# Block 2's experts: rows gathered by index, thirteen weight places, results added to the residual at once

## What is computed

```
def ec_moe(h, w_router, w_gate, w_up, w_down):          # h: 512 tokens x 1024
    cap = EC_FACTOR * T // N_EXPERTS_2                   # 2 * 512 // 16 = 64
    aff = softmax(h @ w_router)                          # 512 x 16
    wts, tok = lax.top_k(swapaxes(aff, 1, 2), cap)       # each expert picks its 64 tokens
    xs = h[bidx, tok]                                    # 16 x 64 x 1024
    hid = silu(xs @ w_gate[e]) * (xs @ w_up[e])          # 1024 x 2048 each
    y = (hid @ w_down[e]) * wts                          # 2048 x 1024
    return zeros_like(h).at[bidx, tok].add(y)

    h2 = modulate(rms_norm(x, norm_ffn_g), sh2, sc2)
    x = x + g2 * ec_moe(h2, ...)
    out = rms_norm(x, norm_final_g)
```

## Time and profile before

| | us |
|---|---|
| median of three runs | 3543.57 |
| lowest and highest run | 3541.1, 3547.78 |
| the profiled execution's own time | 3537.41 |
| its span in the trace | 3535.6 |
| mean granted clock of PE, share of full | 0.92 |

### The profile page before, as it was taken

One profiled execution on the slowest core, in us unless ns is written; L12 is line 12 of the kernel. 1 busy time (PEld: TensorE's weight loads), 2 busy tenths in 40 slices (PEclk: granted clock), 3 DMA queues, 4 the chain that ended last, 5 costly groups with the idle time before them and its releaser, 6 DMA issues.

```text
span 3535.6 us, 34530 instructions
## 1 busy us (share of the span) xinstructions
PE 2982.1 (84%) x14217; PEld 1467.9 (42%) x14217; DVE 989.7 (28%) x1583; ACT 465.0 (13%) x973; POOL 566.5 (16%) x454
## 2 busy tenths in 40 slices
PE   4997699998987899999972697777888888888885
PEld 2644577784444555555531353444222222222221
DVE  2042555553022511111115286722010111111103
ACT  1011222221002111111111102510000000000001
POOL 1001245542001133333320102110000000000000
PEclk6998899999998999999985798887999999999998
DMA  5010144323121399999965210110999999999994
GB/s 212 24 71 0 57 134 127 121 64 149 71 81 63 124 389 401 389 385 386 379 249 215 78 48 32 38 75 0 378 411 402 384 391 398 409 378 398 389 397 203
DMA packets 116883, 786.69 MB, mean 223 GB/s; under 512 B 19532, under 2 KB 19916, under 8 KB 44408
## 3 DMA queue, kind: packets, MB, share of 16 engines
q1 hardware_dynamic: 99256, 741.38, 53.1%
q0 software_dynamic: 15520, 33.60, 2.5%
q10 hardware_dynamic: 1952, 9.50, 0.7%
HBM read 771.22 MB, written 30.47 MB: 227 GB/s over the span
## 4 chain that ended last, share of the span: by engine, by line
PE 68%; DMA 16%; DVE 8%; ACT 3%; issue 3%; POOL 2%; SPq 0%; POOLq 0%; DVEq 0%; ACTq 0%
DMA arena<-in_w_down 12%; PE b L1640 10%; PE b L2649 8%; PE b L1654 5%; PE b L1325 5%; PE b L2198 4%; PE b L472 3%; PE b L474 3%; PE b L2687 3%; PE b L2664 2%; PE b L613 2%; PE b L1045 2%; PE b L1058 2%; PE b L2618 2%; PE b L1362 2%
## 5 line engine op out<-in xcount | busy, mean ns | idle before, releaser
L2649 PE MATMUL b<-arena 128*64 128x512 f32 x2048 | 466.6, 605 | 36.0 <-DMA arena<-in_w_up 21.4
L1640 PE MATMUL b<-arena 128*64 128x256 f32 x3072 | 354.5, 383 | 1.3 <-DVE arena L1916 1.3
L2664 PE MATMUL b<-arena 128*64 128x512 f32 x1024 | 247.7, 606 | 68.5 <-DMA arena<-in_w_down 68.5
L2649 PEld LDWEIGHTS b<-arena 128*64 128x64 f32 x2048 | 139.6, 138 | 366.5 <-issue 263.1
L1640 PEld LDWEIGHTS b<-arena 128*64 128x64 f32 x3072 | 212.3, 136 | 111.8 <-issue 3.1
L1654 PE MATMUL b<-arena 128*64 128x512 f32 x768 | 186.1, 605 | 0.7 <-issue 0.7
L2801 POOL TENSOR_TENSOR arena<-arena 128x256 f32<-128x256 f32 x32 | 19.1, 620 | 1009.5 <-PE b L2676 965.8
L1325 PE MATMUL b<-arena 128*128 128x512 f32 x384 | 167.2, 597 | 9.2 <-DMA arena<-in_w_in 9.2
L1906 DVE TENSOR_TENSOR arena<-arena,b 128x128 f32<-128x128 f32 x96 | 27.8, 290 | 515.8 <-ACT arena L1725 416.2
L2664 PEld LDWEIGHTS b<-arena 128*64 128x64 f32 x1024 | 64.0, 136 | 252.8 <-DMA arena<-in_w_down 151.4
L1940 POOL DMA_INDIRECT yd<-arena x96 | 97.7, 1018 | 391.6 <-ACT arena L1734 383.2
(11 more groups left out here) (464 smaller groups left out, 3857.1 us busy)
## 6 DMA issues: line engine op xcount, KB each, us to landing
arena<-in_w_gu SPq DMA_DIRECT2D x65, 2048.0 KB, 7.8
arena<-in_w_gate SPq DMA_DIRECT2D x128, 1024.0 KB, 14.8
arena<-in_w_up SPq DMA_DIRECT2D x128, 1024.0 KB, 12.3
arena<-in_w_down SPq DMA_DIRECT2D x128, 1024.0 KB, 15.4
arena<-in_w_dn SPq DMA_DIRECT2D x65, 1024.0 KB, 9.8
arena<-in_w_mod SPq DMA_DIRECT2D x80, 512.0 KB, 3.8
arena<-in_w_in SPq DMA_DIRECT2D x17, 2048.0 KB, 8.0
arena<-yd SPq DMA_DIRECT2D x16, 1024.0 KB, 13.5
```

The source lines that it names most:

```text
L1640: x = e.matmul(ps[i % 2][64 * j:64 * j + 64, 0:256], XGT[i % 2][:, k % 4, (k // 4) * 64:(k // 4) * 64 + 64], GUB[w % 3][:, k, j * 256:(j + ...
L2649: x = e.matmul(ps[b + c][64 * hf:64 * hf + 64, :], XS[:, kb, n, :], w[:, q * 512:(q + 1) * 512], start=(kb == 0), stop=(kb == 7), skip_gro ...
L2664: x = e.matmul(ps[4][64 * hf:64 * hf + 64, :], H[:, c * 4 + j, hi * 64:hi * 64 + 64], w[:, i * 1024 + hf * 512:i * 1024 + hf * 512 + 512], ...
```

## The change

Everything is in `experts2`. In an earlier stage only a slice of a constant is written out (the same instruction), and the semaphores of another ring are shared by name.

- **Indices instead of one-hot.** In each round of the search DVE also takes the eight positions (a new instruction between the two). The positions and the affinities, 16 by 64, are turned by six small matmuls into columns: for each expert's slot its token and its weight (ID16, W16), and for each pair of experts 128 tokens (IDP).
- **Gather.** SP writes the normalized rows H2 to a table in HBM (h2d). For each pair of experts POOL gathers 128 rows of 4 KB by index into one of two buffers (XG), PE transposes them (`tokens_T`, eight transposes into the two banks that `back` uses), and ACT and DVE copy one half each to XS. The large one-hot, the matmuls at L2618, and the 32 KB of XS are gone.
- **Thirteen places.** The first seven are free once the attention has ended, and SP fills them then, before the stage opens. The others follow as the norm, the copy of H2 and the router's matmuls end: all thirteen come before the search is over.
- **Back.** DVE multiplies the result of `down` by the gate (G2h) as it leaves its bank, and builds ST from a row of token numbers in one instruction (equal to the slot's token, times its weight). POOL's products, PE's four transposes and ACT's two copies are gone.
- **Residual.** DVE adds straight into X. At the end the square of a tile starts after its own last add, and the scaling of a tile stands between the adds of the following ones.

```
-    slots = [ar(2048) for _ in range(4)]
-    NR = 7
+    early = K.area(K.base1)
+    slots = [early(2048) for _ in range(7)]
+    slots.append(ar(2048))
+    slots.append(K.arena[:, K.R0:K.R0 + 2048])
+    slots += [H2f[:, 0:2048], H2f[:, 2048:4096], H2Tf[:, 0:2048], H2Tf[:, 2048:4096]]
+    NR = len(slots)
...
     def sp(e):
-        opened(e)
-        e.dma_start(wrt, I["w_rt_2"]).then_inc(*came_wr.up())
-        e.dma_start(gfin, I["gfin_2"]).then_inc(*came_gf.up())
+        all_of(e, *K.att)
         for i, (kind, n, q) in enumerate(pieces):
-            if i == 4:
-                e.wait_ge(*mm.at("xs", 7, 1))
+            if i == 7:
+                opened(e)
+                e.dma_start(wrt, I["w_rt_2"]).then_inc(*came_wr.up())
...
+            if i == 8:
+                for t in range(4):
+                    e.wait_ge(*norm.pool.at("ffn2", t))
+                    e.dma_start(K.h2d[t * 128:(t + 1) * 128, :], H2[:, t, :]).then_inc(*kept.up(t))
+            if i == 9:
+                e.wait_ge(*kept.at(3))
+                norm.done(e)
+            if i == 11:
+                e.wait_ge(*mm.at("route", 3))
...
+    def tokens_T(e, q):
+        e.wait_ge(*came_xg[q % 2].at(q))
+        for half in range(2):
+            if q:
+                e.wait_ge(*dve.at("add", 2 * q - 2, 3, half))
+            for j in range(4):
+                x = e.transpose(ps[6 + half][:, hs(j)], XG[q % 2][:, hs(half * 4 + j)], K.ident)
+            x.then_inc(*mm.up("tokens", q, half))
...
-            e.max(TOP, AE).then_inc(*dve.up("best", i))
+            e.max(top, AE).then_inc(*dve.up("best", i))
             e.wait_ge(*dve.now())
-            e.match_replace(AE, TOP, AE, -1.0).then_inc(*dve.up("struck", i))
+            e.max_index(ix, top, AE).then_inc(*dve.up("index", i))
+            e.match_replace(AE, top, AE, -1.0).then_inc(*dve.up("struck", i))
...
+                e.tensor_tensor(Y2[q % 2], ps[4][:, :], G2h, ALU.mult).then_inc(*dve.up("y", q))
+                e.tensor_scalar(ST[q % 2], tokens, ID16[:, q:q + 1], W16[:, q:q + 1], ALU.is_equal, ALU.mult).then_inc(*dve.up("st", q))
...
-                        o = OUT[:, t, hf * 512:(hf + 1) * 512]
+                        o = X[:, t, hf * 512:(hf + 1) * 512]
...
+                    if q == 15 and t:
+                        final(e, t - 1)
...
+        all_of(e, kept)
+        e.wait_ge(*dve.at("pairs"))
+        for q in range(8):
+            if q >= 2:
+                e.wait_ge(*mm.at("tokens", q - 2, 1))
+            e.indirect_dma_start(XG[q % 2], None, K.h2d, off(IDP.bitcast(U32)[:, q:q + 1])).then_inc(*came_xg[q % 2].up(q))
```

More of the change, by code:

```diff
@@ L2060, in combine @@
     came_cx, came_gain = S.dma("cx2"), S.dma("gains2")
-    came_y = [S.dma(f"yrow{i}") for i in range(8)]
+    came_y = [S.dma(f"ring{i}") for i in range(8)]
     dve, act_ = S("comb_dve"), S("comb_act")
@@ L2600, in pe @@
         x.then_inc(*mm.up("affT"))
[L2601 to L2615, removed]
-                    e.wait_ge(*(dve if hf else act_).at("xs", k - 4, hf))
-                for t in range(4):
-                    x = e.matmul(ps[i % 8][:, :], H2[:, t, hs(k)], SS[:, t, hf * 8:hf * 8 + 8, :].rearrange("p e j -> p (e j)"),
-                                 start=(t == 0), stop=(t == 3))
-                x.then_inc(*mm.up("xs", k, hf))
-        e.wait_ge(*act_.at("xs", 7, 0))
-        e.wait_ge(*dve.at("xs", 7, 1))
+        e.wait_ge(*dve.at("indices"))
+        eye = K.ident[0:16, 0:16].rearrange("p (q o) -> p o q", o=2)
+        for o in range(2):
+            r = slice(64 * o, 64 * o + 64)
+            e.matmul(ps[6][r, 0:16], IXf, K.ident[0:16, 0:16], start=True, stop=True, skip_group_check=True)
+            e.matmul(ps[6][r, 16:32], TOPV, K.ident[0:16, 0:16], start=True, stop=True, skip_group_check=True)
+            x = e.matmul(ps[6][r, 32:40], IXf, eye[:, o, :], start=True, stop=True, skip_group_check=True)
+        x.then_inc(*mm.up("columns"))
+        e.wait_ge(*dve.at("columns"))
+        tokens_T(e, 0)
         for n in range(17):
@@ L2656, in down @@
         if n:
-            e.wait_ge(*act_.at("y", n - 1))
+            e.wait_ge(*dve.at("y", n - 1))
         for q in range(8):
@@ L2669, in back @@
     def back(e, n):
[L2670 to L2679 removed]
+        e.wait_ge(*dve.at("st", n))
+        e.wait_ge(*dve.at("y", n))
         for t in range(4):
@@ L2696, in act @@
         e.activation(EXf, EXf, ACT.Exp).then_inc(*act_.up("exp"))
-        for k in range(8):
-            e.wait_ge(*mm.at("xs", k, 0))
-            e.activation(XS[:, k, 0:8, :].rearrange("p e j -> p (e j)"), ps[(2 * k) % 8][:, :], ACT.Copy).then_inc(*act_.up("xs", k, 0))
+        tokens_act(e, 0)
         for n in range(17):
@@ L2773, in dve_, with final @@
                     for hf in range(2):
[L2774 removed]
+                        o = X[:, t, hf * 512:(hf + 1) * 512]
                         e.wait_ge(*mm.at("back", q, t, hf))
[L2776 to L2778 removed]
+                        if q:
                             e.wait_ge(*dve.at("add", q - 1, t, hf))
[L2780 to L2791 removed]
+                        e.tensor_tensor(o, o, ps[6 + hf][:, :], ALU.add).then_inc(*dve.up("add", q, t, hf))
+                    if q == 15 and t:
+                        final(e, t - 1)
+            if n % 2 and n < 15:
+                tokens_dve(e, (n + 1) // 2)
+        final(e, 3)
+    def final(e, t):
+        r = ss2[:, 12 + t:13 + t]
+        e.wait_ge(*act_.at("rms", t))
+        e.reciprocal(r, r).then_inc(*dve.up("rms", t))
+        e.wait_ge(*dve.now())
+        e.wait_ge(*came_gf.end())
+        e.scalar_tensor_tensor(out=X[:, t, :], in0=X[:, t, :], scalar=r, in1=gfin, op0=ALU.mult, op1=ALU.mult).then_inc(*dve.up("final", t))
     def pool(e):
```

153 lines of the change are left out of this document (71 added, 82 removed).

## The result

| | before | after |
|---|---|---|
| median, us | 3542.34 (4 runs, 3533.57 to 3547.78) | 3401.57 (4 runs, 3394.51 to 3403.66) |
| ratio, with 95% interval | | 0.9601 (0.9577 to 0.9626) |
| span of the profiled execution, us | 3535.6 | 3401.8 |
| mean granted clock | 0.92 | 0.925 |

A forecast was written before the change was run, and what follows sets the result against it. It took the weight stream, drained by PE's pauses, as the bound, after a routing that moves nothing. 2431 + 920 + 48.4 = 3399.4, plus 1.8, 3401: -136 against 3537.4, hence 3543.6 - 136 = 3408; range 3391 to 3446.

The forecast's parts named there:

- Term A, routing: From the search to the first gate_up: starts at 2431 us, 52 us earlier, bounds 2426 to 2441.
- The cover: Before the first gather: the table of rows' four writes, sent at about 2370 to 2381, have 40 us to finish.
- Term B, stream: From first gate_up to the landing of expert 14's last down piece: 920 us, 64 less, as PE's pauses stop draining transfers.
- the 3.4, 2 and 1.3 of the sum: Additions to the weight stream: first place freed after a piece at 1.2 GHz 3.4, thin refilling 2, landing 1.3 us.
- 4 us lost each time: Kernel before, each expert: PE's pause leaves the DMA engines without transfers, some 4 us of 63.9 lost.
- PE's need: PE's own work per expert after the change: 53.4 us, under the transfers' 59.8 + 0.7.
- Term C, end: From the landing of expert 14's last down piece to the span's end: 48.4 us, 20 less than 68.6.
- the position row: In the routing's search: finding positions over 512 elements should show at about 0.7 us.
- SP sending without a gap over 3.5 us: SP's queue, once the ring is in use: sends of weights should never be further apart than this.
- (1) A slower full stream: Weight stream slower than 2.493 us a piece: at 2.70, 3483 us, chance 0.05; mild form 3429, within the range.
- (2) PE through its clock: PE becomes the bound at a lower clock: middle form 3445 us, chance 0.08; slow form 3583, chance 0.02.
- (3) Places that help less: SP's in-order ring is held up, so the 4 us an expert stay lost: 3458 us, chance 0.08.

The follow-up runs named there:

- PE + 13.9: Changed kernel with each expert's first down piece multiplied nine times instead of once, 13.9 us more PE work an expert: 3510.8 us, ratio 0.9880 to the kernel before.

## Why the prediction was right, point by point

**The whole.** 3408 was forecast, 3401.6 measured, inside 3391 to 3446. The difference was forecast as -136; the medians give -141, the stretches -137. That the sum came within 1 us of the stretches is luck: the routing and the end gained 5 us more than forecast and the stream 4 less. The bounds as given, added up plainly, would be 3388 to 3445 and not 3391 to 3440; the measured time lies within either.

**Term A, routing: forecast -52, measured 99.7 - 45.0 = -54.7.** Relative to the router's start the first gate matmul was expected at 2431.0 - 2383.3 = 47.7 and came at 45.0. The search for positions over 512 elements takes 0.68 us, near the row I chose (0.67) and far from the 64-element row (0.22, rows 8). A round grew from 1.50 to 2.15 us, so eight cost 5.2 and not 6.4. The six small matmuls, twelve passes, took 1.1 and not 2.7: they started 0.07 us apart and not 0.22, so the ranking matmuls were a poor row to take. From the indices to POOL's gather it was 2424.51 - (2423.52 + 0.17) = 0.8 and from there to PE on the rows 4.5, where 0.8 and 4.3 were forecast from rows 9 and rows 10. The cover held: the first gather waited for DVE and not for the table of rows, whose last write was issued at 2384.0.

**Term B, stream: forecast 920 to the landing of the last down piece of expert 14, -64; measured 3355.8 - 2431.8 = 924.0, -60.** The step that carries it is the one the experiments bear out: a pause of PE no longer reaches the transfers. Its sizes: at the start the sixteenth piece landed 15.4 us after the first gate matmul, where three pieces and the 3.4, 2 and 1.3 of the sum give 14.2. The gathers cost 6.4 and not 8.3. The rest is the pace: in the kernel without later gathers the 360 pieces from there on took 902.1 us, and 360 x 2.493 is 897.5. Its pieces landed 2.49 us apart, but for nine that came 2.7 to 3.3 after the one ahead. Each of the nine stands beside one of the 26 transfers of 16 KB, of the queue that the page lists as "q8 instruction", which hold one of the 16 engines for 1.0 to 1.1 us each. No run takes these transfers away, so that they are the cause is likely and not shown. Together 920 + 1.2 - 1.9 + 4.6 = 923.9.

How the 64.7 us of the stream stretch come about: nine more places at the start 9 x 2.49 = 22.4 by count (8.1 was measured for the three from 10 to 13, 5.4 for the two from 13 to 15; from 4 to 10 the count is not told apart from the drain), less 6.4 for the gathers, and the remaining 49 the filled gaps. Pause by pause the kernel before lacks 51 us, the seven-place kernel 34 and the changed one nothing: so some 32 to 34 go by the depth of the ring and 17 by shorter pauses, fewer of them at the lower clock. "4 us lost each time" was 3.3 an expert by the stretches, and not all of it belonged to the ring.

**PE's need: forecast 53.4 us an expert, measured 52.5** with PE + 13.9, and two errors partly cancel in the forecast: eight down pieces take 13.95 at full clock, not 15.1 (the prediction calls the 15.13 of rows 12 a time at 2.4 GHz, but the granted clock from 3482.0 to 3484.5 was 0.50), and the pause is 11.0 at full clock and 11.44 in the changed trace, not 10.6. In it ST takes 0.54 and not 0.45, and PE waits 1.26 for the first copy of the hidden rows.

**Term C, end: forecast 48.4 from that landing, -20; measured 3401.8 - 3355.8 = 46.0, -22.6.** The pause was 9.8 and not 10.5, down(15) 13.95 and not 15.1. From the start of the last `back` to the last scaling's end it is 3396.6 - 3382.8 = 13.8, forecast 14.2.

**The signs.** The experts took 60.5 us on average, the position row 0.68, the last scaling ended 3.0 behind the last add. One sign was wrong: "SP sending without a gap over 3.5 us". SP still sends nothing for 8.9 to 13.7 us in each pause of PE, since PE frees no place then, however deep the ring:

```profile
3059.84 0.43 SPq L2590 DMA_DIRECT2D arena<-in_w_gate  x1
3069.19 0.33 SPq L2590 DMA_DIRECT2D arena<-in_w_up  x1
```

What changed is that enough pieces are on their way to fill that time: the windows of experts above and the page's slices stand at 420 GB/s all the same. The sign of a ring that is deep enough is the rate, and not the spacing of the sends.

**The rivals.** (1) A slower full stream: the windows stand at 420 GB/s with the gathers in them. The Trainium skill (DMA: Bandwidth & Descriptors, Specifications) puts the limit of HBM for a core at some 358, a stack's 716 halved for two cores. The trace of after holds 420 over 900 us with the kernel on one core, so here the measurement decides; no run here has two cores at it. (2) PE through its clock: windows at 0.95 and 0.96 are as full as those at 1.00, and PE + 13.9 shows what it would have looked like. (3) Places that help less: this was half right in a way that I had not written. The early filling gives nothing, and places beyond ten only what they hold at the start; but ten are enough for all of the rest.

## What to carry to other kernels

When transfers set the time and the consumer pauses, count the pause in transfer times, and leave room above it: seven places hold 17.5 us of transfers and still ran out in pauses of 10 to 15 us; ten, 25 us, never did. What has to be covered is more than the pause: in the kernel before, 13.6 us without a send for a pause of 11.7, and then the time from issue to landing, some 5 us (in the changed kernel the first piece of the stream, issued at 2435.5 with nothing in flight, landed at 2440.7). That makes about 19, by this estimate. A place beyond what this takes is worth only the piece that it holds when the consumer starts. A prefetch moved earlier into idle time is worth nothing if the same places are full in time anyway; a shorter serial path ahead of the first consumer counts in full. To say how much slack an engine has, add work to it until the time moves: what was added less what then shows is the slack.

## What the runs showed of the hardware

With many pieces in flight SP itself is held. The weight issues of gate pieces from 2600 to 3300 us, view of one tile, with the 7-place ring, the 10-place ring, the changed kernel's 13 and the 15-place ring (ns min/median/max):

```profile
L2585 SPq DMA_DIRECT2D arena<-in_w_gate x90: 327/328/328, 2602.8 to 3299.3; - x90
DMA to landing us min/median/max: 6.3/12.7/15.9
```

```profile
L2591 SPq DMA_DIRECT2D arena<-in_w_gate x93: 327/328/328, 2609.1 to 3296.4; - x93
DMA to landing us min/median/max: 10.2/22.8/25.3
```

```profile
L2590 SPq DMA_DIRECT2D arena<-in_w_gate x95: 327/2131/2336, 2605.1 to 3299.3; - x95
DMA to landing us min/median/max: 18.4/27.3/30.4
```

```profile
L2594 SPq DMA_DIRECT2D arena<-in_w_gate x94: 432/2137/2145, 2599.6 to 3293.6; - x94
DMA to landing us min/median/max: 25.8/27.4/29.5
```

The median issue of 1 MiB takes 0.33 us with 7 or 10 places and 2.13 us with 13 or 15. Taken one by one in the changed kernel, an issue took 0.33 us (median) with up to nine pieces out ahead of it and 2.1 or more with ten or more. The time to landing stops growing at 27.4 us, 11 pieces' worth (27.4/2.49). So, as an estimate, ten to twelve such transfers were in flight at most, and SP waited inside its instruction for the rest. It cost nothing here, as SP has only this to do and the engines stayed full; whatever stands behind such an issue in the same queue starts that much later. Why it is so no run shows.

A pause that was 9.8 us long at full clock was 11.7 when the granted clock fell in it (0.79 over the pause), and one of 12.2 was 14.6 (0.77). It fell at different experts in the two traces of the changed kernel; with ten places or more no transfers were missing after such a pause.
